# First attention of a two-layer encoder step: the next group's weights split one turn later

## The reference

```python
def _diff_attn(h, pos, w_in, lq1, lk1, lq2, lk2, sub_g, w_out, lam_init, k_past, v_past):
    q, k, v, g = jnp.split(h @ w_in, 4, axis=-1)
    q = _rope(q.reshape(b, t, A_HEADS, 2, A_DH), pos)
    k = _rope(k.reshape(b, t, A_HEADS, 2, A_DH), pos)
    ...
    def block(qb, qpb):
        s = jnp.einsum('bqhcd,bkhcd->bhcqk', qb.astype(f32), kf) * (A_DH ** -0.5)
        mask = k_chunk[None, :] <= (qpb // CHUNK)[:, None]
        pr = jax.nn.softmax(jnp.where(mask, s, NEG_INF), axis=-1)
        w = pr[:, :, 0] - lam * pr[:, :, 1]
        return jnp.einsum('bhqk,bkhe->bqhe', w, vf)
    o = _sweep(block, q, pos)
    o = _rmsnorm(o, sub_g) * (1.0 - lam_init)
    o = o.reshape(b, t, A_WIDTH).astype(h.dtype) * jax.nn.silu(g)
    return o @ w_out, k, v
```

## Time and profile before

| what | value |
|---|---|
| median of 3 runs | 2099.2 us (2097.88 to 2100.6) |
| the profiled execution | 2100.87 us, of which 2099.1 us is the span |
| TensorE busy in the span | 1921.5 us (92%) |
| mean granted TensorE clock | 0.965 |
| first attention, seven looped groups | from about 61 to 650 us, some 85 us each |

### The profile page before, as it was taken

One profiled execution on the slowest core, in us unless ns is written; L12 is line 12 of the kernel. 1 busy time (PEld: TensorE's weight loads), 2 busy tenths in 40 slices (PEclk: granted clock), 3 DMA queues, 4 the chain that ended last, 5 costly groups with the idle time before them and its releaser, 6 DMA issues. The chain is left out here.

```text
span 2099.1 us, 35461 instructions
## 1 busy us (share of the span) xinstructions
PE 1921.5 (92%) x11429; PEld 1645.4 (78%) x11429; DVE 1254.7 (60%) x2661; ACT 998.6 (48%) x2356; POOL 323.7 (15%) x541
## 2 busy tenths in 40 slices
PE   4998999999999899997799999999999999889996
PEld 4877878778778699996677777777777777679996
DVE  5446455564554632454287868686868687854555
ACT  5445454454554532454254545455545455532335
POOL 0111111111111100364011101010101111100341
PEclk9999999999999999998899999999999999989999
DMA  4111111111211242211111111111101011233213
GB/s 156 49 61 36 45 46 57 59 36 45 66 47 50 93 117 79 65 65 56 39 47 37 46 36 46 36 46 36 52 30 55 27 56 39 80 102 98 63 39 132
DMA packets 161892, 124.22 MB, mean 59 GB/s; under 512 B 11137, under 2 KB 152769, under 8 KB 161793
## 3 DMA queue, kind: packets, MB, share of 16 engines
q1 hardware_dynamic: 160928, 122.88, 19.1%
q10 hardware_dynamic: 864, 0.20, 0.0%
HBM read 89.53 MB, written 33.52 MB: 59 GB/s over the span
## 5 line engine op out<-in xcount | busy, mean ns | idle before, releaser
L107 PE MATMUL pj<-area,h_high 128*128 128x384 f32 (+1 forms) x2304 | 669.6, 353 | 26.3 <-DVE lb_qk_low L1347 6.9
L107 PEld LDWEIGHTS pj<-area,h_high 128*128 128x128 f32 (+1 forms) x2304 | 415.9, 185 | 51.0 <-DVE lb_qk_low L1347 8.6
L107 PE MATMUL pj<-area,h_low 128*128 128x384 f32 (+1 forms) x1152 | 395.6, 343 | 0.0
L107 PEld LDWEIGHTS pj<-area,h_low 128*128 128x128 f32 (+1 forms) x1152 | 214.2, 186 | 8.7
L1197 ACT ACTIVATE lb_m<-lb_m 128x512 f32<-128x512 f32 (+4 forms) x200 | 98.8, 521 | 236.7 <-DVE lb_m L1358 235.5
L1535 POOL TENSOR_TENSOR lb_o<-lb_o,lb_keep 128x512 f32<-128x512 f32 (+3 forms) x80 | 77.5, 969 | 646.5 <-ACT lb_keep L1221 644.0
L1371 DVE TENSOR_TENSOR lb_s<-lb_sc,lb_m 128x512 f32<-128x512 f32 (+4 forms) x200 | 110.0, 550 | 61.4 <-ACT lb_m L1202 61.2
L456 ACT ACTIVATE la_p<-la_sc,la_nm 128x128 f32<-128x128 f32 (+5 forms) x144 | 106.2, 739 | 62.0 <-DVE la_nm L653 60.1
L1358 DVE TENSOR_SCALAR lb_m<-lb_sc 128x512 f32<-128x512 f32 (+4 forms) x200 | 101.3, 545 | 37.2 <-PE lb_sc L1613 22.3
L1410 DVE TENSOR_TENSOR lb_s_low<-lb_s,lb_s_high 128x512 fp32r<-128x512 f32 (+1 forms) x192 | 113.5, 591 | 7.1
L651 DVE TENSOR_REDUCE la_mx<-la_sc 128x1 f32<-128x128 f32 (+5 forms) x144 | 107.6, 747 | 2.9
(11 more groups left out here) (308 smaller groups left out, 4469.0 us busy)
## 6 DMA issues: line engine op xcount, KB each, us to landing
stage<-in_a_w_in SPq DMA_DIRECT2D x60, 192.0 KB, 2.9
stage<-in_b_w_in SPq DMA_DIRECT2D x60, 192.0 KB, 2.6
stage<-in_ple_w_gate SPq DMA_DIRECT2D x22, 512.0 KB, 3.7
h_low<-o_t SPq DMA_DIRECT2D x14, 528.0 KB, 6.5
mix_b_xs<-x_mid SPq DMA_DIRECT2D x8, 528.0 KB
lift_xt<-in_x SPq DMA_DIRECT2D x8, 512.0 KB, 4.4
stage<-in_a_w_in SPq DMA_DIRECT2D x16, 256.0 KB, 5.4
out_ak<-la_tok SPq DMA_DIRECT2D x8, 512.0 KB, 3.3
```

Of the source, the lines that this page charges most:

```text
L107: last = pe.matmul(out, x, y, start=start and n == 0, stop=stop and n == 2, **kw)
```

## The change

The splits of the next group's weights are issued in turns 10, 11 and 12 instead of 9, 10 and 11, on ScalarE and VectorE alike. On ScalarE `move(8, 0)` of turn 12 is put behind the splits of that turn, and the wait for `pj_tok` goes with the first split.

```diff
@@ -269,7 +269,7 @@
     LAST = 13
     GATE_AT = {9: 0, 10: 1, 11: 2}
     PAST_AT = 6
-    WEIGHTS_AT = {9: range(0, 3), 10: range(3, 6), 11: range(6, KT)}
+    WEIGHTS_AT = {10: range(0, 3), 11: range(3, 6), 12: range(6, KT)}
     GATE_WEIGHTS_AT = {12: 0, 13: 1}
     BLOCKS_AT = {12: range(0, 2), 13: range(2, 4)}
     OUT_AT = {9: 0, 10: 1}
@@ -542,13 +542,15 @@
                         act.activation(kpt[0][:, :], past_bank, ACT.Copy).then_inc(S["past_high"], 1)
                     if j == 9:
                         norm(0)
-                    if 0 <= j - 4 <= NT:
+                    if 0 <= j - 4 <= NT and j != 12:
                         move(j - 4, 0)
                     if more and j in WEIGHTS_AT:
-                        if j == 9:
+                        if j == 10:
                             act.wait_ge(S["pj_tok"], at.all("pj_tok"))
                         for k in WEIGHTS_AT[j]:
                             split_w(r + 1, k)
+                    if j == 12:
+                        move(j - 4, 0)
                     if more and j == 13:
                         turned_high(ahead, 0)
                     if j == 13:
```

## The result

The changed kernel takes 2125.56 us (median of 4 runs, 2125.24 to 2125.77) against 2098.56 for the kernel before (4 runs): 27.0 us more, a ratio of 1.0127 with a 95% interval of 1.0109 to 1.0144. The profiled span grew from 2099.1 to 2123.7 us, by 24.6. Nearly all of the 2.4 us between the two differences comes from the profiled execution of before, which at 2100.87 us was 2.3 slower than the median.

What follows compares the result with a forecast made beforehand. TensorE, 92% busy, was taken to bound the kernel through its waits and clock. Five groups at +3.7 us and two at +1.73 made +22 on 2100.87: 2122.9, likely median about 2122; own range 2112 to 2130, stated range 2109 to 2131.

Steps and rivals of the forecast that it cites:

- the first gap: TensorE's wait for `probs` of block 7 ahead of the scores of unit 8: to shrink from 2.83 to some 0.3 us.
- The second gap: TensorE's wait for `combine(7)` ahead of `turn_weights(7, 0)`: to grow from 1.66 to about 3.3 us.
- the third: New TensorE wait in LATE for the splits of tiles 6 and 7: some 3.4 us in each of seven groups.
- (a): Turns 10 and 11: block 7's maxima through `turn_weights(7, 0)` come 2.58 us earlier per group, 0.43 more saved in two groups.
- (b): EARLY in turn 12 runs at the low clock in every group: 1.54 us more in five, nothing new in two.
- (c): LATE in turn 12 waits for tiles 6 and 7, split behind the gate work: 3.2 us more in all seven groups.
- (d): `values(1)`, behind LATE's new wait, runs at the low clock: 1.54 us more per group in all seven.
- The first rival: In the looped groups the clock adds nothing, so each costs only +0.6 us: 2103 us, chance 0.09.
- the rival on the faster side: LATE's wait doesn't come, as tiles 6 and 7 are ready in time: -11.2 us, 2088 us, chance 0.04.
- The third rival: In turn 10 something else holds block 7's maxima until 281.85, so the 2.58 us are missing: 2132 us, chance 0.03.

Runs made afterwards that it cites:

- experiment 6: The changed kernel with GpSimd's gate product of piece 2 held back until the split of tile 7 is done: 2121.37 us.
- experiment 5: The changed kernel with turn 12's splits put ahead of the gate work on ScalarE and VectorE: 2095.17 us, ratio 0.9978 to the kernel before.
- experiment 3: The changed kernel with 15 matmuls that nobody reads between tiles 5 and 6 of LATE: 2115.59 us.
- experiment 9: The changed kernel with unread matmuls in two places, 12 ahead of `turn_weights(7, 0)` and 15 between tiles 5 and 6 of LATE: 2106.84 us.
- experiment 1: The kernel before with only the splits of tiles 6 and 7 moved to turn 12, tiles 0 to 5 left in turns 9 and 10: 2149.68 us.
- experiment 4: The changed kernel with 12 matmuls that nobody reads ahead of `turn_weights(7, 0)`: 2121.57 us.
- experiment 10: The kernel before with 12 matmuls that nobody reads ahead of the scores of unit 8 in turn 10: 2107.57 us, ratio 1.0034.
- experiment 8: The changed kernel with tiles 0 to 3 split in turn 10, 4 to 7 in turn 11, plus 12 unread matmuls ahead of `turn_weights(7, 0)`: 2084.03 us.
- experiment 7: The changed kernel with tiles 0 to 3 split in turn 10, 4 to 7 in turn 11 and none in turn 12: 2094.08 us.

## Why the prediction was right, step by step

The direction and the place came as forecast, and every wait of the forecast was there at about its size: 0.26 us for the first gap, 3.0 for the second, 3.6 for the third. The whole was 4 to 5 us short, +27.0 measured against +22 to 23. What follows sets the terms of the sum against the third group, the one they were made for.

- (a) The maxima of block 7 started right behind the normalization, as forecast. From it to `turn_weights(7, 0)` it is 299.43 - 285.31 = 14.12 us against 295.53 - 278.58 = 16.95: a gain of 2.83, predicted 2.58. The other 0.25 come from transposes of block 6 ahead of ScalarE's move and splits, which in that group before were at low clock (0.96 us, now 0.65). The second gap was 2.98 us, predicted 3.3.
- (b) EARLY: +1.55 us, predicted 1.54, and low in all groups, in the first only in part (0.74).
- (c) LATE: +4.11 us (6.22 against 2.11), predicted 3.2. The chain on ScalarE and VectorE was right: VectorE's first split began 307.79 - 304.11 = 3.68 us behind the transposes, forecast 3.69. Three things were missing. That split took 0.975 us instead of 0.55 since GpSimd's product ran beside it; experiment 6 removed this. The matmuls of tiles 6 and 7 take 1.25 us at full clock (experiment 6) where the prediction had some 1.04, that is 0.2 more. And here they ran partly at the low clock: 310.33 - 308.81 = 1.52 us, 0.27 more.
- (d) From `turn_weights(8, 0)` to the end of `values(1)`: 317.60 - 310.33 = 7.27 us. Before, the next product began at 306.77 (row below), 6.00 behind the 300.77 of the earlier trace rows; so +1.27, predicted 1.54. With the 0.27 us inside LATE the fall costs 1.5 us in this group. Over all seven it is some 12 us, and experiment 5 confirms that.

```profile
306.77 0.42 PE L107 MATMUL pj<-area,h_high 128*128 128x384 f32 x1
```

The four terms give -2.83 + 1.55 + 4.11 + 1.27 = +4.1 us for this group, predicted 3.7. Over six groups, from the scores of unit 8 in the first to those in the seventh, the mean is +3.7: 85.3 us before, 89.0 after, as these rows show (first before, then after).

```profile
114.13 0.63 PE L847 MATMUL la_sc<-la_kpt_high,la_qk_high 64*32 64x512 f32 x2 [2.83 <-ACT la_p L456]
```

```profile
626.05 0.64 PE L847 MATMUL la_sc<-la_kpt_high,la_qk_high 64*32 64x512 f32 x2 [2.83 <-ACT la_p L456]
```

```profile
111.36 0.42 PE L849 MATMUL la_sc<-la_kpt_high,la_qk_high 64*32 64x512 f32 x2 [0.26 <-ACT la_p L456]
```

```profile
645.64 0.41 PE L849 MATMUL la_sc<-la_kpt_high,la_qk_high 64*32 64x512 f32 x2 [0.26 <-ACT la_p L456]
```

The same stretches over all seven groups, added up from TensorE's rows of both kernels (us):

| term | before | after | measured | predicted |
|---|---|---|---|---|
| (a) first gap, and from the scores of unit 8 to `turn_weights(7, 0)` | 87.1 | 65.5 | -21.6 | -18.9 |
| (b) to `turn_weights(7, 1)` | 25.0 | 32.0 | +7.0 | +7.7 |
| (c) to `turn_weights(8, 0)` | 14.7 | 44.9 | +30.2 | +22.4 |
| (d) to the next product | 42.0 | 50.8 | +8.8 | +10.8 |
| sum | | | +24.4 | +22.0 |

The sum fits the 24.6 us between the spans. The term that was sized wrong is thus (c), by 7.8 us. That the total missed by only 2.4 us in the profiles is partly luck, since (a), (b) and (d) erred the other way by 2.7, 0.7 and 2.0 us.

The error in (a) is a reading of the rows of before. The prediction had the low clock on the chain, 9.78 us from the scores to `turn_weights(7, 0)`, in groups two and seven alone. The trace has 9.78 us in groups one, two, five, six and seven, and 9.10 in all seven groups of the changed kernel; so 0.68 us was saved in five groups, not 0.43 in two. The sixth group before, as one of those that the prediction left out (550.58 - 540.80 = 9.78):

```profile
540.80 0.63 PE L847 MATMUL la_sc<-la_kpt_high,la_qk_high 64*32 64x512 f32 x2 [2.83 <-ACT la_p L456]
...
550.58 0.66 PE L864 MATMUL la_third<-ident,la_p 128*128 128x128 f32 x4 [1.25 <-DVE la_p L666]
```

One working of the prediction doesn't come out either: clock terms of 7.7 + 10.8 us at two thirds or one and a half times give 2116 to 2131, not 2112 to 2130.

The first rival, that the clock adds nothing, is refuted by experiments 3, 5 and 9: with the clock held at 1.00 the changed kernel loses 6 us, not 27. Its own estimate for that case, +3.5 us, lacked among other things the 0.43 us of the collision with GpSimd (3 us in seven groups). The rival on the faster side needed a short wait in LATE; experiment 5 shows it was right in kind, since with the wait at 1.2 us the kernel is faster than before. The third rival is refuted by (a).

One part of the reasoning was too simple though it did no harm: falls of the clock were added as independent terms. Experiments 1, 4 and 10 show that they are not. A fall that is taken away lengthens the next wait or the next fall. What exactly decides how long a fall lasts stays open; the runs show only that it varied by place and by group.

The Trainium skill, "TensorE: Matmul & The Clock Gate", under "HAM oscillation", describes a kernel in which each wait makes the work behind it start at the low clock, so that the wait costs a second time. Experiments 3, 5 and 9 agree, with 11, 12 and 21 us. Experiment 10 doesn't: there a wait was filled and the kernel became slower.

## What to carry to other kernels

When a step is moved later to clear the way for another, count the engine's queue at the new place, from the instruction that it now stands behind to the instruction that reads its result: here 2.6 us won in turn 10 were paid with 3.6 in turn 12, because two splits came to stand behind gate work that waits for three engines in turn. A gap of TensorE has a second price in the clock behind it, but whether that price is paid depends on whether the next stretch has another wait to hide it. So look for the next wait before filling or removing one, and time the combination, not each part.

## What the runs showed that I had not expected

A VectorE subtraction with both operands in SBUF took 0.975 us instead of 0.55 whenever it began inside GpSimd's 0.93 us product, in each of seven groups: it began at 307.79, the product ended at 307.42 + 0.93 = 308.35, and the split ended at 308.76. That is 0.41 us behind the product, less than the 0.55 of a whole split, so the rows don't settle whether it stood still for all of the overlap. "SBUF — State Buffer" of the Trainium skill says under "Who interferes with whom" that a VectorE instruction with two inputs in SBUF gets its second input through the read interface that it shares with GpSimd, and so contends with a GpSimd instruction that reads SBUF. Experiment 6 (0.549 to 0.560 us for all sixty, once the two were kept apart) agrees.

Matmuls that nobody reads made a kernel 10 us faster (experiment 8 against 7) in one place and another 7 us slower (experiment 10 against before).
